# A hybrid encoder trunk on one core: dilated q, k and v leave PSUM by class, and v comes back from DRAM in 8 loads

## The reference

```python
def hybrid_layer(x, g, w_in, rpb, w_dw, b_dw, ln_g, ln_b, w_pw, b_pw, w_out, pos):
    h = rms_norm(x, g)
    z = h @ w_in
    aq, ak, av, ag, bq, bk, bv, bg, ca, cb, cg = jnp.split(z, splits, axis=-1)
    ya = neighbourhood_attention(heads(aq, 4), heads(ak, 4), heads(av, 4), rpb) * silu(ag)
    yb = dilated_attention(rotary(heads(bq, 6), pos), rotary(heads(bk, 6), pos), heads(bv, 6)) * silu(bg)
    yc = conformer_conv(ca, cb, w_dw, b_dw, ln_g, ln_b, w_pw, b_pw) * silu(cg)
    return x + jnp.concatenate([ya, yb, yc], axis=-1) @ w_out
```

## Time and profile before

| what | value |
|---|---|
| median of 3 runs | 541.35 us (537.8 to 543.76) |
| the profiled execution | 539.04 us, its span 537.3 us |
| mean granted clock of TensorE | 0.981 |
| TensorE, products | 508.9 us busy, 95% of the span |
| VectorE | 366.4 us, 68% |
| ScalarE | 244.6 us, 46% |
| GpSimd | 163.7 us, 30% |
| DMA | 99.75 MB, mean 186 GB/s |

### The profile page before, as it was taken

The page is one execution under the profiler, slowest core; times in us unless marked ns, Lnnn a source line. Parts: engine busy times, 40 slices in busy tenths (PEclk is TensorE's granted clock), DMA queues, the critical chain, the costliest instruction groups (busy, mean ns, idle before and its releaser), DMA issues.

```text
span 537.3 us, 10125 instructions
## 1 busy us (share of the span) xinstructions
PE 508.9 (95%) x3902; PEld 410.3 (76%) x3902; DVE 366.4 (68%) x733; ACT 244.6 (46%) x483; POOL 163.7 (30%) x224
## 2 busy tenths in 40 slices
PE   8999999699799999999999999987989999999995
PEld 7888877587587777778888888766868777787884
DVE  6879787589786486621558968974998667653325
ACT  6712365246355565522543114642654655653224
POOL 0104232112023556533521223222212425664201
PEclk9999999799899999999999999997999999999998
DMA  8725789848879698999613367985698879999973
GB/s 293 279 78 135 153 214 225 172 94 178 200 178 212 139 252 202 222 236 292 147 41 98 99 137 177 225 172 115 151 227 177 206 174 274 232 209 248 227 181 156
DMA packets 61263, 99.75 MB, mean 186 GB/s; under 512 B 24480, under 2 KB 38304, under 8 KB 61216
## 3 DMA queue, kind: packets, MB, share of 16 engines
q0 software_dynamic: 19648, 62.93, 52.8%
q1 hardware_dynamic: 41280, 36.00, 23.0%
q10 hardware_dynamic: 288, 0.19, 0.1%
HBM read 84.92 MB, written 4.72 MB: 167 GB/s over the span
## 4 chain that ended last, share of the span: by engine, by line
PE 77%; DMA 7%; DVE 6%; issue 5%; POOL 2%; SPq 1%; ACT 1%; POOLq 0%; DVEq 0%; ACTq 0%
PE acc L625 17%; PE acc L626 16%; PE acc L627 16%; DMA sq<-sq 4%; PE sc L734 4%; PE tp L767 3%; PE misc L798 3%; DMA w_hi<-w_in 2%; PE misc L793 1%; PE sc L687 1%; DMA w_lo<-w_out 1%; PE sc L688 1%; PE sc L689 1%; SPq L505 1%; PE sc L625 1%
## 5 line engine op out<-in xcount | busy, mean ns | idle before, releaser
L625 PE MATMUL acc<-act_hi,w_hi 128*128 128x512 f32 x480 | 194.5, 405 | 0.0
L626 PE MATMUL acc<-act_hi,w_lo 128*128 128x512 f32 x480 | 187.6, 391 | 0.0
L627 PE MATMUL acc<-act_lo,w_hi 128*128 128x512 f32 x480 | 187.2, 390 | 0.0
L625 PEld LDWEIGHTS acc<-act_hi,w_hi 128*128 128x128 f32 x480 | 90.2, 188 | 21.9 <-issue 3.9
L627 PEld LDWEIGHTS acc<-act_lo,w_hi 128*128 128x128 f32 x480 | 90.2, 188 | 19.9
L626 PEld LDWEIGHTS acc<-act_hi,w_lo 128*128 128x128 f32 x480 | 90.3, 188 | 17.0 <-issue 0.5
L893 ACT ACTIVATE w_lo<-w_hi 128x1024 fp32r<-128x1024 f32 (+1 forms) x62 | 62.0, 1000 | 66.1 <-DMA w_hi<-w_out 39.1
L1318 DVE SCALAR_TENSOR_TENSOR y<-ub,par,y 128x512 f32<-128x512 f32 x90 | 68.5, 761 | 0.0
L1096 POOL DMA_DIRECT2D w_lo<-w_in x40 | 36.1, 901 | 100.2 <-ACT w_lo L893 99.6
L955 ACT ACTIVATE prob<-prob,nmx 128x384 f32<-128x384 f32 (+1 forms) x80 | 45.2, 565 | 45.4 <-DVE nmx L1340 45.4
L1318 DVE SCALAR_TENSOR_TENSOR ub<-ub,par 128x512 f32<-128x512 f32 x84 | 62.6, 745 | 0.0
(11 more groups left out here) (147 smaller groups left out, 720.7 us busy)
## 6 DMA issues: line engine op xcount, KB each, us to landing
w_hi<-w_in POOLq DMA_DIRECT2D x40, 512.0 KB, 5.9
w_lo<-w_in POOLq DMA_DIRECT2D x40, 512.0 KB, 6.1
w_hi<-w_out POOLq DMA_DIRECT2D x16, 512.0 KB, 6.2
w_lo<-w_out POOLq DMA_DIRECT2D x16, 512.0 KB, 6.6
pT<-w_in SPq DMA_DIRECT2D x15, 512.0 KB, 3.6
sq<-sq SPq DMA_DIRECT2D x48, 64.0 KB, 4.0
gf<-nabias SPq DMA_DIRECT2D x20, 128.0 KB, 5.6
v_way<-vs SPq DMA_DIRECT2D x32, 64.0 KB, 4.1
```

Source lines behind the costliest of these rows:

```text
L625: nc.tensor.matmul(to[:, :], w_hi[:, slot, k, :], a_hi[:, k, :], start=i == 0, stop=False)
L626: nc.tensor.matmul(to[:, :], w_lo[:, slot, k, :], a_hi[:, k, :], start=False, stop=False)
L627: last = nc.tensor.matmul(to[:, :], w_hi[:, slot, k, :], a_lo[:, k, :], start=False, stop=i == K - 1)
```

## The change

- bq and bk leave PSUM by `scaled_by_class` in place of `scaled`, so they are in class order from the start, and so are `zs`, `zsw`, `zc` and the rotary table on the host. `rotated` then adds contiguous operands: for k all of it, for q in runs of 32 with the blocks reordered.
- `take_factor` makes a second copy of the factor, `rstd_c`, in class order, read from PSUM with a step of 4. `scaled_by_class` takes its factor from there, contiguously; PSUM is still read with a step of 4.
- For a dilated pair VectorE turns `vT` twice: once as before (512 columns), once shifted by half a block (3 blocks in each class, 384 columns). `vB` and `v_way` grow from 512 to 896 columns; the stores are still 4 for a pair.
- `load_v` issues 2 DMAs for each quarter of the partitions, near keys (896 bytes a piece) and far keys (128 bytes a piece, as before): 8 for a dilated pair. Local pairs are loaded as before.
- All pairs share `vB`, and each bv or av tile waits until the stores of the pair before have landed.

```diff
--- before.py
+++ after.py
@@ -166,10 +166,10 @@
         keys = sb("k", [P, 2, SEQ])
         v = sb("v", [P, 2, 4, NA_BLOCKS * BLK])
         v_far = sb("v_far", [P, 2, 4, CLASSES * BLK])
-        vs = sb("vs", [P, 2, SEQ])
-        vT, vB = vs[:, 0, :], vs[:, 1, :]
-
-        v_way = nc.dram_tensor("v_way", (DEPTH, PAIRS, BLK, P // BLK, SEQ), F32, kind="Internal").ap()
+        vs = sb("vs", [P, SEQ + CLASSES * NA_BLOCKS * BLK])
+        vT, vB = vs[:, 0:SEQ], vs[:, SEQ:]
+
+        v_way = nc.dram_tensor("v_way", (DEPTH, PAIRS, BLK, P // BLK, CLASSES * NA_BLOCKS * BLK), F32, kind="Internal").ap()
         zc = sb("zc", [P, 2, SEQ])
         ub = sb("ub", [P, CT * (SEQ + 2 * HALO) + SEQ])
         u = ub[:, 0:CT * (SEQ + 2 * HALO)].rearrange("p (j t) -> p j t", j=CT)
@@ -187,6 +187,7 @@
         zs, zsw = sq[:, 0, :], sq[:, 1, :]
         ssq = sb("ssq", [P, SEQ])
         rstd = sb("rstd", [P, SEQ])
+        rstd_c = sb("rstd_c", [P, SEQ])
         cnt = sb("cnt", [P, QT * DKEY])
         cs = sb("cs", [P, 2, SEQ])
         ident = sb("ident", [P, P])
@@ -388,13 +389,12 @@
 
 
         QUADS = P // BLK
-        NEAR_EVEN, NEAR_ODD = slice(0, QT * BLK), slice(QT * BLK, NA_BLOCKS * BLK)
 
         V_STORED = 16 * QUADS
 
         def v_moves(g):
 
-            return 4 * QUADS if g < DPAIRS else QUADS
+            return 2 * QUADS if g < DPAIRS else QUADS
 
         def v_landed(l, g):
 
@@ -413,15 +413,13 @@
         X_MOVES = {27 + i: (0, i) for i in range(QUADS)}
         X_MOVED = 16 * QUADS * QUADS
 
-        def v_buf(g):
-
-            return zs if g == 1 else vB
-
-        def v_blocked(g):
-
-            if g < DPAIRS:
-                return v_buf(g).rearrange("p (m j t) -> p m j t", j=QUADS, t=BLK)
-            return v_buf(g).rearrange("p (z m t) -> p m z t", z=2, t=BLK)
+        def by_chunk(t):
+
+            return t.rearrange("p (r m t) -> p r m t", r=CLASSES, t=BLK)
+
+        def v_columns(g):
+
+            return CLASSES * NA_BLOCKS * BLK if g < DPAIRS else SEQ
 
         def by_class(t):
 
@@ -447,7 +445,7 @@
 
         def p_turned(q):
 
-            return (prob[:, 2:4, :], sq, vs, zc)[q][:, :, :].rearrange("p r t -> p (r t)")
+            return vs[:, 0:2 * SEQ] if q == 2 else (prob[:, 2:4, :], sq, None, zc)[q][:, :, :].rearrange("p r t -> p (r t)")
 
         def p_there(q):
 
@@ -507,7 +505,8 @@
             def store_v(l, g):
                 sp.wait_ge(v_blocks, PAIRS * l + g + 1)
                 for i in range(QUADS):
-                    sp.dma_start(v_way[l, g, :, i, :], v_buf(g)[BLK * i:BLK * (i + 1), :]).then_inc(v_stored, 16)
+                    n = v_columns(g)
+                    sp.dma_start(v_way[l, g, :, i, 0:n], vB[BLK * i:BLK * (i + 1), 0:n]).then_inc(v_stored, 16)
 
             def load_v(l, g):
                 sp.wait_ge(v_stored, V_STORED * (PAIRS * l + g + 1))
@@ -516,19 +515,14 @@
                 for j in range(QUADS):
                     to = v[BLK * j:BLK * (j + 1), g % 2]
                     if g < DPAIRS:
-                        half = BLK // 2
-                        low = NEAR_ODD.stop - NEAR_ODD.start
-                        t = v_way[l, g].rearrange("p i (j c) -> j p i c", j=QUADS)
-                        sp.dma_start(to[:, :, NEAR_EVEN], t[j]).then_inc(v_moved[g % 2], 16)
-                        sp.dma_start(to[0:half, :, NEAR_ODD], t[j][half:BLK, :, 0:low]).then_inc(v_moved[g % 2], 16)
-                        sp.dma_start(to[half:BLK, :, NEAR_ODD], t[j][0:half, :, BLK:BLK + low])\
-                            .then_inc(v_moved[g % 2], 16)
-                        t = v_way[l, g].rearrange("p i (r j c) -> j p (i r) c", r=CLASSES, j=QUADS)[j]
+                        t = v_way[l, g].rearrange("p i (r c) -> r p i c", r=CLASSES)[j]
+                        sp.dma_start(to[:, :, :], t).then_inc(v_moved[g % 2], 16)
+                        t = v_way[l, g].rearrange("p i (r m c) -> m p (i r) c", r=CLASSES, c=BLK)[j]
                         sp.dma_start(v_far[BLK * j:BLK * (j + 1), g % 2].rearrange("p i (r c) -> p (i r) c", r=CLASSES), t)\
                             .then_inc(v_moved[g % 2], 16)
                     else:
                         first = BLK * (j // 2)
-                        t = v_way[l, g].rearrange("p i (z c) -> z p i c", z=2)[j % 2]
+                        t = v_way[l, g, :, :, 0:SEQ].rearrange("p i (z c) -> z p i c", z=2)[j % 2]
                         t = t[:, :, first:first + BLK * NA_BLOCKS]
                         sp.dma_start(to[:, :, 0:BLK * NA_BLOCKS], t).then_inc(v_moved[g % 2], 16)
 
@@ -1203,7 +1197,8 @@
 
             def take_factor(l):
                 dve.wait_ge(misc_ready, MISC_L * l + MISC_BC + 1)
-                nc.vector.tensor_copy(rstd[:, :], misc[:, :]).then_inc(misc_free, 1)
+                nc.vector.tensor_copy(rstd[:, :], misc[:, :])
+                nc.vector.tensor_copy(by_class(rstd_c[:, :]), in_order(misc[:, :])).then_inc(misc_free, 1)
                 dve.wait_ge(misc_free, MISC_L * l + MISC_BC + 1)
 
             def scaled(dst, c, factor):
@@ -1222,7 +1217,7 @@
             def scaled_by_class(dst, c, factor):
 
                 return nc.vector.scalar_tensor_tensor(out=by_class(dst), in0=in_order(bank_of(c)[:, :]), scalar=factor,
-                                                      in1=in_order(rstd[:, :]), op0=ALU.mult, op1=ALU.mult)
+                                                      in1=by_class(rstd_c[:, :]), op0=ALU.mult, op1=ALU.mult)
 
             def empty_tile(l, c):
 
@@ -1240,7 +1235,7 @@
                     nc.vector.scalar_tensor_tensor(out=mid, in0=mid, scalar=1.0, in1=half, op0=ALU.add,
                                                    op1=ALU.mult).then_inc(u_ready, 1)
                 elif kind in ("bq", "bk"):
-                    scaled(zs, c, HD ** -0.5 if kind == "bq" else 1.0).then_inc(acc_free, 1)
+                    scaled_by_class(zs, c, HD ** -0.5 if kind == "bq" else 1.0).then_inc(acc_free, 1)
                     dve.wait_ge(acc_free, emptied(l, c))
 
                     is_k = kind == "bk"
@@ -1255,11 +1250,17 @@
                     (scaled_by_class if kind == "bv" else scaled_by_column)(vT, c, 1.0).then_inc(acc_free, 1)
                     dve.wait_ge(acc_free, emptied(l, c))
 
-                    before = {0: (l - 1, PAIRS - 1), 2: (l, 0), 3: (l, 2), 4: (l, 3)}.get(g)
-                    if before is not None and before[0] >= 0:
-                        dve.wait_ge(v_stored, V_STORED * (PAIRS * before[0] + before[1] + 1))
-                    nc.vector.transpose(v_blocked(g), vT.rearrange("p (m j t) -> p m j t", m=v_blocked(g).shape[1],
-                                                                         t=BLK)).then_inc(v_blocks, 1)
+                    before = PAIRS * l + g
+                    if before:
+                        dve.wait_ge(v_stored, V_STORED * before)
+                    if g < DPAIRS:
+                        nc.vector.transpose(by_chunk(vB)[:, :, 0:QT, :], vT.rearrange("p (r m t) -> p r m t", r=CLASSES, t=BLK))
+                        shifted = vT.rearrange("p (r a) -> p r a", r=CLASSES)[:, :, BLK // 2:P - BLK // 2]
+                        nc.vector.transpose(by_chunk(vB)[:, :, QT:NA_BLOCKS, :],
+                                            shifted.rearrange("p r (m t) -> p r m t", t=BLK)).then_inc(v_blocks, 1)
+                    else:
+                        nc.vector.transpose(vB[:, 0:SEQ].rearrange("p (z m t) -> p m z t", z=2, t=BLK),
+                                            vT.rearrange("p (m z t) -> p m z t", z=2, t=BLK)).then_inc(v_blocks, 1)
                 elif kind == "aq":
 
                     def by_block(a):
@@ -1278,13 +1279,12 @@
                 dve.wait_ge(dve_own, own[0])
                 z = zc[:, r % 2, :]
                 if r % 2:
-                    to = by_class(keys[:, r // 2 % 2, :])
-                    ins = nc.vector.tensor_tensor(to, in_order(z), in_order(zsw), ALU.add)
+                    ins = nc.vector.tensor_tensor(keys[:, r // 2 % 2, :], z, zsw, ALU.add)
                 else:
-                    def by_block(a):
-                        return a.rearrange("p (b a r) -> p b r a", b=QT, r=CLASSES)
+                    def by_tile(a):
+                        return a.rearrange("p (r b a) -> p b r a", b=QT, r=CLASSES)
                     to = queries[:, r // 2 % 2, :].rearrange("p (b r a) -> p b r a", b=QT, r=CLASSES)
-                    ins = nc.vector.tensor_tensor(to, by_block(z), by_block(zsw), ALU.add)
+                    ins = nc.vector.tensor_tensor(to, by_tile(z), by_tile(zsw), ALU.add)
                 ins.then_inc(qk_ready, 1)
 
             def turn_blocks(half):
@@ -1623,6 +1623,7 @@
     ang = np.arange(SEQ)[None, :] * 10000.0 ** (-np.arange(half) * 2.0 / HD)[:, None]
     cos, sin = np.cos(ang), np.sin(ang)
     out = np.stack([np.tile(cos, (4, 1)), np.concatenate([-sin, sin, -sin, sin])], 1)
```

(1 more changed line is left out.)

## The result

The changed kernel takes 524.84 us (median of 4 runs, 522.79 to 526.76) against 540.85 us for the kernel before beside it: a ratio of 0.9704, interval 0.9638 to 0.9770. Timed again it took 523.45 us, 0.9644 (0.9557 to 0.9731). So it is 3.0 to 3.6% faster by these ratios, which leave out every execution over 1.5% above the fastest of its kernel, as the medians do not (the second timing's medians alone give 0.967). The forecast was 518.0 us with a range of 515 to 531, and the range held. The profiled execution took 526.76 us, its span 525.0 us, 12.3 us less than the span before; it is the longest of its four.

A forecast was written before the change was run, and what follows sets the result against it. Bound: TensorE's `values` stalls, awaiting v's last load. Removing 22.25 us from the 537.3 us span gives 515.05, 516.8 with 1.7 us around it, 519.1 from the median; forecast 518.0 between the two, range 515 to 531.

The forecast's parts named there:

- A: Rival for `values` of dilated pairs: all four TensorE stalls go, 515 to 522 us; chance 0.70.
- B: Rival: half of 22.25 us comes back, 530 us; chance 0.16, 0.10 for late loads (first form), 0.06 for the DVE.
- The bound: TensorE's four waits at `values`, 17.0 us, no releaser named, were put down to v's last load; 22.25 us excess together.
- The tail of a stall: After a stall at `values` the granted clock is 0.50, so following products run slowly; 5.2 us beyond the 17.0 us.
- leave each landing as it was: Last loads issued 6.0 us sooner, landing times unchanged: v in time at four `values` calls by 0.8, 2.0, 0.3, 4.0 us.
- W: Theory from the experiments, not the prediction: a last load issued just behind GpSimd's issues of a tile's weights lands late.
- The bounds I gave: If loads take 6.85 us to land everywhere, pairs 0 are late at `values` by 0.5 and 1.2 us.
- The way to the store: DVE scaling and turning before a dilated pair's store, 0.26 us sooner; first store to first load, +0.3 us.
- upper bound of 4.1 us: Growth of a pair's first-store-to-first-load gap, 5.5 to 9.6 us, if the larger store goes by its bytes.
- None is on TensorE's path: Other VectorE work (rotary sums, v scalings, transposes, factor copies), together -2.5 us, at upper bounds +5.5, doesn't hold up TensorE.
- C: Rival: v's transfer, not its issue, is the bound; 8 loads land no sooner, 541 us (537 to 545); chance 0.08.
- D: Rival: the larger store delays loads, pairs 1 wait 4.1 us longer, pairs 0 about 2; 553 us; chance 0.06.

The follow-up runs named there:

- 16 loads: The changed kernel with each of a dilated pair's 8 loads cut in two, same bytes by 16 loads: 533.97 us, 0.985 of the kernel before.
- ScalarE's detour: The changed kernel with the four far loads issued by ScalarE's queue, the near ones by SyncE's: 530.43 us, 0.980 of the kernel before.
- less weights: The changed kernel with one eighth of the rows in the low-weight loads of tiles 15 and 16, layer 0: 525.05 us, 0.964 of the kernel before.
- class order only: The kernel before plus class-order PSUM reads with the second factor; one transpose, 64 KB stores and 16 loads kept: 538.40 us, 0.993.
- loads-only kernel: The changed kernel with q, k and v leaving PSUM as before; second transpose, wider store and 8 loads kept: 521.41 us, 0.963 of the kernel before.
- 5-load kernel: The changed kernel with dilated stores laid out by class, near keys in one load, 5 loads for 8: 518.73 us, 0.956 of the kernel before.

## Why the prediction was right and where it was not

*What the range could tell.* It took in A, all four stalls gone, and B, half of it back. The time, 524.84 us, lies between A's 515 to 522 and B's 530, so the range held without deciding between them, and 518.0 was 6.8 us too low.

*The bound, right.* The four waits without a releaser were the wait for v's last load. With half the issues two of them are gone, putting the issues back restores all four (16 loads), and the kernels whose profile has none of them, ScalarE's detour apart, have spans of 516 to 520 us.

*The tail of a stall, right.* Behind the stall of 5.17 us the window of 101 to 102 us is granted 0.50 again,

```profile
101.00:102.00 1.00, 0.19 (x5) 0.22 (x9) 0.22 (x2) 0.00 (x0) 0.00 (x0) 0.50 1.12 127
```

and pair 0's near part takes 3.41 us for 1.75. Behind the 2.49 us none of it is seen: its excess is 2.56 us. The length of the stall does not settle it: in other runs one of 2.65 us had the tail (less weights, pair 1 of layer 0, granted 0.50 behind it) and one of 3.62 us had none (class order only, pair 1 of layer 1, granted 1.00).

*The term that was mis-sized: "leave each landing as it was".* The margins of 0.8, 2.0, 0.3 and 4.0 us rested on it. At pair 0 of layer 0 the last load went out 5.5 us sooner but took 10.1 us to land in place of 5.5, and TensorE came 0.8 us sooner: the stall is 5.2 us again. At pair 1 of layer 1, with the largest margin, the last load went out 15.2 us sooner and took 2.3 us longer to land, while TensorE came 13.3 us sooner. I had read the dip of the earlier trace rows, DMA share 0.45, as room into which the loads would drain. In the changed kernel that stretch reads

```profile
91.00:93.00 2.00, 2.00 (x10) 1.62 (x9) 2.00 (x4) 0.78 (x2) 1.32 (x2) 1.00 1.15 229
```

with a share of 1.15: the dip was a gap that the transfers happened to leave, and no room to count on. Low weights were issued at 86.08 in the changed kernel, 83.86 before, and the next two weight loads at nearly the same time in both (91.22 and 91.80 before); which of them filled the gap was not tried. The bounds I gave (0.5 and 1.2 us late) came from the longest landing of a last load in the trace of before, 6.85 us. What makes a landing take 10 us is shown in part: with the weights held back the same load landed in 3.2, but W's pattern does not always bring a late landing. So 10.3 of the 22.25 us stayed in that execution. Others had more or less of it: the kernel's executions spread over 519 to 530 us, where the loads-only kernel's lie within 1.1 us.

*The way to the store, right in the DVE, wrong in the gap.* I took +0.3 us from the first store to the first load; it was 2.2 and 2.7 us more for pairs 1 (7.7 for 5.5, 8.1 for 5.4). The upper bound of 4.1 us held. It had its part in both stalls that are left. The first load of pair 0 used to follow the swaps at once (85.00); now it waited 1.3 us for the stores to land, and went out at 86.28 although the stores were issued 0.7 us sooner. The loads of pair 1 of layer 1 began only 9.8 us sooner (375.43 for 385.20) where TensorE came 13.3 us sooner, and 2.7 of these 3.5 us are the gap; its stall is 2.49 us.

*"None is on TensorE's path", wrong in its parts.* The prices were right and what they do to TensorE was taken at 0. For the change as a whole that came out: TensorE waits 2.0 us for turned tiles, for 2.3 before. But the class order by itself gave 0.7%, and without it the 5-load kernel loses some 4 us by the ratios, at the turned tiles. With 8 loads no such loss shows in the time: the loads-only kernel, 0.963, is no slower than the changed one, 0.970 and 0.964. Its TensorE waits 5.8 us for ScalarE's tiles, half a microsecond of it the load's, but has hardly a stall for v. The chain would be DVE, ScalarE, TensorE: a reciprocal or an emptied tile that comes sooner lets ScalarE turn a tile sooner. I looked for the DVE's slack at its wait before `gated`, behind `values`; that says nothing of the slots ahead of it. The last link is read from the waits, the rest is argued; that each of the 4 us went this way was not tried.

*The rivals.* C and D did not occur as accounts of the whole, though at the two stalls that are left the transfer and the slower store had their part. The profiled execution is B's: about half came back, by its first form, late loads, but late by 5.2 us at one pair 0 and by 2.5 us at a pair 1, not by one or two at pairs 0. I gave this form 0.10 and A 0.70. The best of the eight executions, 518.96 us, is A's. That the range held is in part luck: how much comes back hangs on what the last loads and the stores meet in the queues, which the sum did not foresee.

*By the Trainium skill*, SBUF — State Buffer, section "Door 1: The DMA port swizzle", PSUM read in steps of 16 bytes should have been slower. The section says this of matmuls, and I had carried it over to VectorE. The trace does not bear it out there: 681 ns for 678.

## What to carry to other kernels

When a wait ends a few microseconds behind the last of many small DMAs, count the issues: fewer of them took 3 to 4% off here with more bytes moved. But a margin smaller than the spread of a landing is no margin; look at what else is issued near that load, in other queues too, and at the store ahead of it, and leave it the longest landing you have seen (10 us here), not the median. An engine with 30% idle can still stand in the path in the slots where its work feeds another.

## What the runs showed of the hardware

- The last 64 KB load of a pair landed in 3.2 and 2.6 us (5-load kernel: 4.2 twice) with the weight loads of GpSimd's queue held back until it had landed, and in 10.1, 9.8 and 9.4 us in three of four cases behind two loads of 512 KB that this queue had issued at most 1.4 us earlier, in the fourth in 5.1. Elsewhere it took 2.6 to 8.9 us.
- One load of 448 KB with 3584 bytes a partition was issued in 0.35 us and landed in 5.9 us (median of 6), where each of the four of 112 KB took 0.5 us or more to issue and landed in 4.9 us (median of 40, the local pairs' loads among them).
- VectorE read PSUM in steps of 16 bytes at the contiguous rate, 681 ns for 512 columns. The 1076 ns of before came from the SBUF operand: it alone was made contiguous.
- Behind a stall of TensorE of 5.17 us its granted clock was 0.50; behind one of 2.65 us as well, behind others of 2.49 and 3.62 us it was not.
